# Input and output projections of a two-layer recurrent trunk: fp32 matmuls, or three fp32r products of split operands

## The reference, cut to what matters

```python
h = _rmsnorm(x, norm_mix_g[l]) * (1 + sc1) + sh1
p = h @ w_in          # even layer: 1024 x 3848; odd layer: 1024 x 4096
...                   # even: q|k (1024 columns), v (512), o (512), gates (8), RWKV (1792); odd: q, f, i, g of 1024 each
out = mixed @ w_out   # 1024 x 1024 in both layers
x = x + g1 * out
```

## Time and profile before

| | us |
|---|---|
| median of 3 runs (lowest, highest) | 4790.65 (4787.81, 4792.71) |
| the profiled execution | 4791.16 |
| its span, first to last instruction | 4789.2 |
| PE busy | 4496.2 (94%) |
| DVE, ACT, POOL busy | 2921.7, 1858.8, 1384.6 |
| mean granted TensorE clock | 0.971 of full speed |

### The profile page before, as it was taken

How to read it: one execution, slowest core, us unless ns; L and a number is a source line. 1 busy time by engine, 2 the same in 40 slices (tenths; PEclk the granted TensorE clock), 3 DMA queues, 4 the chain that set the end, 5 groups by cost and what they waited for, 6 DMA issues and landing times. The chain is left out here.

```text
span 4789.2 us, 62064 instructions
## 1 busy us (share of the span) xinstructions
PE 4496.2 (94%) x23999; PEld 3597.0 (75%) x23999; DVE 2921.7 (61%) x4501; ACT 1858.8 (39%) x4023; POOL 1384.6 (29%) x581
## 2 busy tenths in 40 slices
PE   8997699989999999999999978898999999999998
PEld 6666486868887888888877547686887788888887
DVE  2045743699985636666651059369997563666665
ACT  1011121138876843222220023114887684322222
POOL 0000000034354544444430000003435454444443
PEclk9997899999999999999999998899999999999999
DMA  4231203226686665545532150223668666555553
GB/s 161 86 117 44 71 30 107 72 89 185 173 256 178 185 203 200 198 180 198 198 130 75 53 158 1 95 61 101 178 178 257 177 182 199 200 198 191 188 198 118
DMA packets 522581, 702.23 MB, mean 147 GB/s; under 512 B 47065, under 2 KB 407122, under 8 KB 501810
## 3 DMA queue, kind: packets, MB, share of 16 engines
q1 hardware_dynamic: 514692, 680.69, 44.1%
q0 software_dynamic: 4608, 16.78, 1.1%
q10 hardware_dynamic: 2990, 0.82, 0.1%
HBM read 548.95 MB, written 145.01 MB: 145 GB/s over the span
## 5 line engine op out<-in xcount | busy, mean ns | idle before, releaser
L2543 PE MATMUL ps<-h_parts,u_parts 128*128 128x512 f32 x6144 | 1457.3, 394 | 21.9 <-POOL u_parts L1991 15.3
L2543 PEld LDWEIGHTS ps<-h_parts,u_parts 128*128 128x128 f32 x6144 | 1154.5, 191 | 259.0 <-POOL u_parts L1991 26.6
L1991 POOL TENSOR_TENSOR u_parts<-u_turned,u_parts 128x1024 fp32r<-128x1024 f32 x256 | 708.2, 2766 | 2039.1 <-ACT u_parts L1986 2039.1
L2807 PE MATMUL ps<-w_parts,v_parts 128*128 128x512 f32 x4080 | 938.8, 389 | 0.0
L2807 PEld LDWEIGHTS ps<-w_parts,v_parts 128*128 128x128 f32 x4080 | 766.1, 188 | 158.7
L215 PE MATMUL ps<-h,arena 128*128 128x264 f32 (+2 forms) x2176 | 484.6, 386 | 18.6 <-PEq L487 16.7
L1978 DVE STREAM_TRANSPOSE u_turned<-u_rows 128x1024 f32<-128x1024 f32 x256 | 317.3, 1240 | 280.3 <-POOL u_parts L1991 193.6
L2807 PE MATMUL ps<-first_w,first_v 128*128 128x512 f32 x2064 | 482.0, 389 | 6.6 <-PEq L2468 6.6
L215 PEld LDWEIGHTS ps<-h,arena 128*128 128x128 f32 (+1 forms) x2176 | 411.0, 189 | 92.5 <-issue 22.0
L2807 PEld LDWEIGHTS ps<-first_w,first_v 128*128 128x128 f32 x2064 | 387.4, 188 | 87.6 <-issue 7.4
L2426 DVE TENSOR_TENSOR onehots<-iota,choice 128x1024 fp32r<-128x1024 f32 x256 | 430.1, 1694 | 0.1
(11 more groups left out here) (532 smaller groups left out, 5116.3 us busy)
## 6 DMA issues: line engine op xcount, KB each, us to landing
u_rows<-in_peer_u_dram SPq DMA_DIRECT2D x1024, 128.0 KB, 3.4
u_rows<-in_peer_v_dram SPq DMA_DIRECT2D x86, 1024.0 KB, 4.9
hidden_tiles<-hidden SPq DMA_DIRECT2D x256, 256.0 KB, 2.2
gate_matrices<-h SPq DMA_DIRECT2D x64, 1024.0 KB, 6.2
gates<-gate_matrices SPq DMA_DIRECT2D x32, 2048.0 KB, 8.0
u_turned<-hidden_tiles SPq DMA_DIRECT2D x256, 256.0 KB, 3.3
arena<-in_ada_w_dram SPq DMA_DIRECT2D x48, 1024.0 KB, 5.4
v_rows<-in_peer_v_dram SPq DMA_DIRECT2D x42, 1024.0 KB, 4.9
```

Source lines behind the costliest of these rows:

```text
L1991: s.nc.gpsimd.tensor_tensor(q.uTs[:, n % 3, 1], q.uT[:, n % 2], q.uTs[:, n % 3, 0].bitcast(F32), ALU.subtract).then_inc(q.u_ready.sem, 1)
L2543: ins = mm(ps[:, n % 2, :], q.uTs[:, n % 3, wp, k, :], q.hs[:, xp, k, :], start=k == 0 and (wp, xp) == (0, 0), stop=k == DT - 1 and wp == 1)
L2807: ins = nc.tensor.matmul(ps[:, o, :], q.vs[n % 3][:, vp, o * P:(o + 1) * P], q.ws[n % 3][:, wp], start=n == 0 and (vp, wp) == (0, 0), stop ...
```

## The change

All four projections are made of **units** of 128 weight columns. For each unit ACT rounds the raw fp32 weights to fp32r (high part), DVE subtracts it from the raw ones (low part); both lie in a double buffer. h is split the same way once for each stage. For each of the 8 feature tiles PE multiplies high x high, low(w) x high(h) and high(w) x low(h), all fp32r, on both halves: 48 matmuls a unit. In the stage's first two units all products with high(h) come first. The value columns become units too: their tiles are drained feature-major to a two-slot stage tile, turned by five PE transposes (`turned_tile`) and drained again to v. The two gate tiles become one unit. Raw weights come in blocks of 256 columns (1 MB; the first two 128) into a ring of three; a block's slot is free once its last unit is split. `ahead`, the adaLN loads, uses the same ring (its own ring of 2 or 3 slots is gone) and so waits for its slots' last splits. In `mix_norm` the scale and shift of the prompt columns is gone; `split_stage` does it while splitting. The clearing of `e.rw` by POOL moves from `even_projection` to `even_mix`. The sample columns are added to x at the end of the projection's Block.

```diff
+RAW = 3
+BEGUN = 2
+class Projection:
+    def load(self, sp, b):
+        if b >= RAW:
+            sp.wait_ge(s.w_low.sem, s.w_low.at(self.last[b - RAW] + 1))
+        for at, a, z in self.blocks[b]:
+            sp.dma_start(s.raw[:, b % RAW, :, at:at + z - a], ...)
+    def free(self, sp, slot):
+        last = max(b for b in range(len(self.blocks)) if b % RAW == slot)
+        sp.wait_ge(self.s.w_low.sem, self.s.w_low.at(self.last[last] + 1))
+    def high(self, act, i, through=None):
+        act.wait_ge(s.weights[b % RAW].sem, s.weights[b % RAW].at(self.there(b)))
+        if i >= 2:
+            act.wait_ge(s.filled.sem, s.filled.at(through[i - 2]))
+        s.nc.scalar.copy(s.parts[:, i % 2, 0], self.of(i)).then_inc(s.w_high.sem, 1)
+    def low(self, dve, i):
+        dve.wait_ge(s.w_high.sem, s.w_high.at(i + 1))
+        s.nc.vector.tensor_tensor(s.parts[:, i % 2, 1], self.of(i), s.parts[:, i % 2, 0].bitcast(F32),
+                                  ALU.subtract).then_inc(s.w_low.sem, 1)
+def split_stage(s, proj, groups, normed, ahead=None, pool_first=None, dve_later=None, drained=None):
...
+            def by_high(i, unit, first=False):
+                for k in range(DT):
+                    if first:
+                        pe.wait_ge(s.h_high.sem, s.h_high.at(k + 1))
+                    for w in range(2):
+                        for j in range(2):
+                            nc.tensor.matmul(slot(i)[:, j, 0:HALF[j + 1] - HALF[j]], s.parts[:, unit % 2, w, k, :],
+                                             hh[:, 0, k, part(j)], start=k == 0 and w == 0, stop=False)
+            def by_low(i, unit, first=False):
+                for k in range(DT):
+                    if first:
+                        pe.wait_ge(s.h_low.sem, s.h_low.at(k + 1))
+                    for j in range(2):
+                        ins = nc.tensor.matmul(..., s.parts[:, unit % 2, 0, k, :], hh[:, 1, k, part(j)], ...)
+                ins.then_inc(s.filled.sem, 1)
+            if normed:
+                pe.wait_ge(s.h_side.sem, s.h_side.at(1))
+            for unit in range(BEGUN):
+                pe.wait_ge(s.w_low.sem, s.w_low.at(unit + 1))
+                by_high(unit, unit, unit == 0)
+            for unit in range(BEGUN):
+                by_low(unit, unit, unit == 0)
...
+        def _(act):
+            if not normed:
+                proj.high(act, 0)
+            for k in range(DT):
+                if normed:
+                    ins = nc.scalar.activation(hh[:, 0, k, 0:T], h[:, k, 0:T], ACT.Identity, bias=..., scale=...)
+                else:
+                    ins = nc.scalar.copy(hh[:, 0, k, :], h[:, k, :])
+                ins.then_inc(s.h_high.sem, 1)
+                if k == 3 and not normed:
+                    proj.high(act, 1)
...
+            for i, (unit, _, who, drain) in enumerate(groups):
+                if unit is not None and unit and unit + 1 < len(proj.units):
+                    proj.high(act, unit + 1, through)
+                if who == "act":
+                    act.wait_ge(s.filled.sem, s.filled.at(i + 1))
+                    drain(nc.scalar, slot(i)).then_inc(s.act_drained.sem, 1)
...
+def turned_tile(s, source, stage, dst, c0, who):
+    def turn(ps):
+        for t in range(TT):
+            s.nc.tensor.transpose(ps[:, 0, t * P:(t + 1) * P], stage[:, t * P:(t + 1) * P], s.ident[:])
+        return s.nc.tensor.transpose(ps[0:B, 1, 0:P], stage[:, T:N], s.ident[:])
...
 def mix_norm(s, layer, proj, mods=None):
+            if not mods:
+                proj.high(act, 0)
             act.wait_ge(s.sum_ready.sem, s.sum_ready.at(1))
...
             if mods:
                 mods.on_act(act, units)
-            act.wait_ge(s.gain_ready.sem, s.gain_ready.at(1))
-            for k in range(0, DT, 2):
-                act.wait_ge(s.xn_ready.sem, s.xn_ready.at(k + 1))
-                a.activation(h[:, k, 0:T], h[:, k, 0:T], ACT.Identity, bias=shift[:, k, 0:1], scale=s.modA[:, k, 0:1])
+                proj.high(act, 0)
+            proj.high(act, 1)
...
+            if not mods:
+                proj.low(dve, 0)
             dve.wait_ge(s.root_ready.sem, s.root_ready.at(2))
...
             if mods:
+                proj.low(dve, 0)
                 dve.wait_ge(s.mod_done.sem, s.mod_done.at(mods.count))
...
-            for k in range(1, DT, 2):
-                v.tensor_scalar(h[:, k, 0:T], h[:, k, 0:T], s.modA[:, k, 0:1], shift[:, k, 0:1], ALU.mult, ALU.add)
```

More of the change, by code:

```diff
@@ L113, in give, with tiles_stage @@
             self.arena.give(self.places.pop(i)[1])
[L121 to L126, removed]
+def tiles_stage(s, groups, banks=1, begin=None):
     nc = s.nc
@@ L182, in _ @@
                 begin.act(act)
[L183 removed]
+            for i, (_, who, drain) in enumerate(groups):
                 if who == "act":
@@ L205, in copy @@
     return nc.scalar.copy(out, in_) if eng is nc.scalar else nc.vector.tensor_copy(out, in_)
[L208 to L214, removed]
-                ins = s.nc.tensor.matmul(ps[0:m, h, 0:z - a], w[:, k, c0:c0 + m], src[:, k, a:z],
-                                         start=k == 0, stop=k == kt - 1)
-        return ins
-    return (b, fill, engine, drain)
@@ L492, in _ @@
                 mods.load(sp, i)
-            load_blocks(s, sp, blocks[0:RING])
+            for b in range(RAW):
+                proj.load(sp, b)
         @block.scalar
@@ L1040, in _ @@
         def _(sp):
-            load_blocks(s, sp, blocks)
+            for b in range(RAW if proj else 0):
+                proj.load(sp, b)
         @block.scalar
@@ L1121, in drain_of @@
         return drain
-    groups = [feature_tile(s, k // 4, (k % 4) * P, P, s.h, "dve", drain_of(k), kt) for k in range(DT)]
-    tiles_stage(s, groups, banks=2, blocks=blocks, loaded=2)
-    with nc.Block() as block:
-        @block.vector
-        def _(dve):
-            nc.vector.tensor_tensor(s.x[:, :, T:N], s.x[:, :, T:N], s.tmp8[:], ALU.add)
+    split_stage(s, proj, [(k, None, "dve", drain_of(k)) for k in range(DT)], False,
+                drained=lambda v: v.tensor_tensor(s.x[:, :, T:N], s.x[:, :, T:N], s.tmp8[:], ALU.add))
 def block_masks(s, pool, bd, sizes):
@@ L1836, in _ @@
                 e.mods.load(sp, i)
-            load_blocks(s, sp, column_blocks(s.io["even_w_out"][0]))
+            for b in range(RAW):
+                s.proj.load(sp, b)
         @block.tensor
@@ L2921, in masked, with ahead @@
         hgrn_masks(s, o, dve)
-    begin.pool, begin.dve = cleared, masked
-    begin.sp = begin.act = begin.pe = lambda engine: None
-    tiles_stage(s, groups, banks=2, blocks=column_blocks(w), begin=begin, loaded=RING,
-                ahead=lambda sp: [o.mods.load(sp, i) for i in range(2)])
+    def ahead(sp):
+        for i in range(2):
+            s.proj.free(sp, i)
+            o.mods.load(sp, i)
+    split_stage(s, s.proj, groups, True, ahead, cleared, masked)
     s.block_made.close(len(LEVELS) - 1)
```

345 lines of the change are left out of this document (241 added, 104 removed).

## The result

| | before | after |
|---|---|---|
| median us (lowest, highest) | 4790.43 (4787.81, 4792.71), 4 runs | 4682.28 (4678.03, 4687.65), 4 runs |
| the profiled execution | 4791.16 | 4678.03 |
| its span | 4789.2 | 4676.3 |
| mean granted clock | 0.971 | 0.971 |

The ratio of after to before is 0.9775, with a 95% interval of 0.9758 to 0.9792. The forecast of 4686 is 4 us above the median, inside the spread of the kernel's own runs, and 8.5 above the profiled execution; the range held both.

A forecast was written before the change was run, and what follows sets the result against it. PE's matmul stream was taken to bound the projections: 587.7 us before, less 468.6 for the new stream and 14.4 at stage edges, saves 104.7, so 4791.2 - 104.7 = 4686.5 us; range 4646 to 4723.

The forecast's parts named there:

- The price of a matmul: In the projections' PE stream: 120 ns per 256-column fp32r matmul, 123.3 for 264 columns, so 5.84 us a unit.
- The gap formula of the Trainium skill: For matmul spacing in projections: columns/2.4 + 2.5 ns whatever the type, 109 and 113 ns, a unit of 5.32 us.
- Rival (a): In the projections the fp32 gap applies, weight load of 112 ns as floor: 36 us less, 4650; chance 0.08.
- The overlap rule: Loads overlap running matmuls only where row groups differ; projections use the full array, so the kernel would take 5055 us.
- rival (c): In the projections weight loads come out from under the matmuls: slower, 4823 at 158 ns, 5055 end to end; chance 0.04.
- Feeding the units: In the projections drain, cast, subtract and hand-overs take 3.6 us inside a 5.84 us unit: cost nothing, cover 2.2.
- Rival (b): In the projections a DVE or ACT stall makes the split pace units at 6.3 us: 4723, up to 4745; chance 0.10.
- DMA and `ada_w`: Weight blocks stay hidden and adaLN loads after the projections arrive in time: cost 0, bounds 0 and 5 us per layer.
- POOL's clearing: Clearing the rw tile moves into even_mix beside DVE: cost 0, at most 2.3 us.
- Edges: Losses at projection starts and ends: odd input 2.1, even input 3.7, outputs 4.3 each, 14.4 us in all.
- late link: At the odd input's start, cast 2 waits for unit 0 to fill and its Silu drain; PE waits about 1.3 us.
- the ramp: At the odd input's start, the half-speed clock, partly hidden under ACT's pace, was taken to cost 0.8 us.

## Why the prediction was right, step by step

- **The price of a matmul.** 120 ns from the burst of the earlier trace rows held for 3792 of them: 120.2. The 264-column matmul costs some 2 ns more by the start times in the trace, not the 3.3 of the slope. A unit is 5.77 for 5.84, 79 x 0.07 = 5.5 us in all; this and the turned tiles (0.47 for 0.60, 1.6 us) are what the forecast missed of the stream.
- **The gap formula of the Trainium skill** (TensorE: Matmul & The Clock Gate, Back-to-back issue gap), 109 and 113 ns, does not give the step here: the unit would be 5.32, and it is 5.77. The section itself gives this formula for isolated matmuls and says that in a stream in which each matmul has its load the spacing is another; the prediction left that out. Rival (a) falls, though a floor exists: 213 ns at the lower clock, and 111.7 was the shortest step at the upper one, with 192 columns.
- **The overlap rule** of the same page (What overlaps and what doesn't), which made 5055 by rival (c), is contradicted: 48 full-array weight loads pass under 48 matmuls in 5.77 us, and at the lower clock the step with 256 columns is their 213 ns and no more. The bursts of the earlier trace rows had shown it in groups of eight and 24; it holds for thousands.
- **Feeding the units** cost nothing, as written. The reason was right, the chain mis-sized: 2.6 and 3.1 us in turn for 3.6, a cover of 3.2 and 2.7 for 2.2. A doubled subtraction is hidden, a fourfold one is not. Rival (b) needed the chain to be slowed by more than 2.7 us a unit.
- **DMA and `ada_w`**: right for layer 0, no DMA wait after the even projection. In layer 1 PE waits for `ada_w` four times, 6.8 us in all, as it did before the change (7.6).
- **POOL's clearing**: the step that was wrong, taken at 0 with 2.3 as its bound, costs 1.4 in its stage. DVE beside POOL was the row to distrust: L2747's 2.45 us of the earlier trace rows had pointed to it.
- **Edges**: 14.4 forecast. Measured as what is missing between stream and stage, 587.7 - 79 x 5.77 - 12 x 0.47 - 109.0 = 17.2: even input 3.6 (for 3.7), odd input 3.4 (2.1), outputs 4.4 and 5.6 (4.3 each). The odd input's late link is 1.04 (1.3 forecast); what was too small is the ramp, 0.8, as the forecast let ACT's pace hide part of it: 64 products take 9.91 us there, 2.2 more than 7.7. The odd output's idle of 3.44 us is followed by 10.61 us at a mean granted clock of 0.72, the even one's of 3.10 us by 9.46 at 0.82.

The stream was 7.1 us better and the edges 2.8 worse than forecast, so the projections gave 109.0 and not 104.7. The executions' difference of 113.1 us and that of the medians, 108.2, lie around it: `even_mix` took 1.4 back, and the rest, 5.3 in the profiled ones, is stages that the change doesn't touch. So the mechanism and the price of its main term were right, but that the median came out within 4 us is in part luck: errors of 7.1, 2.8 and 1.4 us went different ways, and the profiled execution missed by twice as much.

## What to carry to other kernels

Read the price of a new stream from a burst of the same operation in the old trace, not from a single instruction's duration: 120 ns against the 287 of the earlier trace rows. In a chain of cast, subtraction and matmul, size the cover by the slowest engine's unit; doubling one link on purpose shows what is left of it. And before work is moved ahead of a barrier, look at what ends the stage on that engine and whether its data have landed: the same two casts, with a third part buffer, saved 3.6 us behind `head_norm`'s roots, cost 2.8 at the end of `rwkv_output`, and 7.7 in its middle, against 2.9 won in the projection.

## What the runs showed of the hardware

- fp32r matmuls that moved only 128 columns each ran at a granted clock of 0.50 (1.2 GHz) through all four projections, 331 and 352 us in the two input stages, with PE busy for 15.00 of 15.00 us in the stretch shown; with 192 columns the clock was back at 1.00 some 6 us after the start. Half the work took 1.7 times as long (866 for 510 us in the projections).
- With 128, 192 or 248 moved columns a matmul with its own weight load took 213 ns, 256 cycles, at the lower level, and with 192 or 248 it took 112 to 115 ns at the upper.
- Whether the clock falls in a PE idle time of 2.05 us depends on more than that time: 2.05 us left it at 1.00, 2.06 us in another kernel ended at 0.50, for 1.69 us, and in a third 1.98 us ended at 0.50 and 2.06 us at 1.00. Edits of one or two microseconds drown in this; they can be seen in a stage's time, and not in a median of five.
- A POOL memset of 2080 columns (1.83 us) held up DVE's small copies beside it until it ended, 1.96 us instead of 0.5; in the projection, where the splits have at least 2.7 us of slack a unit, the stage took 189.5 us for 189.2.
